# Two transformer layers on one core: the banks of the MLP down phases are copied by ScalarE and added by GpSimd's DMAs, and a fourth pair takes seven products

## The chip, the core and the metric

The kernel runs on one core of a Trainium2 chip. TensorE (PE) multiplies, VectorE (DVE) and ScalarE (ACT) work on vectors, GpSimd (POOL) and SyncE (SP) here mostly issue DMAs. The metric is the device time of one execution in microseconds, the median of several runs. A lower time is better.

## What is computed

Two different layers follow each other on x of 256 tokens by 2048 channels, all in float32. This case is about the MLP that ends each layer:

```python
x = x + jnp.square(jax.nn.relu(h @ w_mlp_up[l])) @ w_mlp_down[l]     # first_block, h = rms_norm(x)
...
u = rmsnorm(x, g_mlp) @ w_up                                          # hybrid_layer
return x + jnp.square(jax.nn.relu(u)) @ w_down
```

The hidden width is 8192. Ahead of the MLP stand, in the first layer, an attention, a gated recurrence and a short convolution, and in the second a state-space part and an attention with a top-k choice. The change leaves them alone.

## The kernel before

All weights come as one stream of 938 chunks of 512 KB (128 x 1024 floats). SP loads a chunk into one of four raw slots as soon as DVE is done with the chunk four before it. ACT rounds the chunk to `whi` (L614), and DVE makes the rest, `wlo` = raw - whi (L1104). PE multiplies with three matmuls for each product (high by high, high by low, low by high), which gives nearly float32 accuracy. `prep(c)` on ACT and on DVE always prepares chunk c+4, and whi of a chunk waits until PE is done with the chunk four before it (`mm_done`). Each engine runs its instructions in the order of the program.

An MLP is cut into four groups of hidden columns (`FF_GROUPS`), g = 0 to 3. In a group, 32 chunks make 16 hidden tiles (up), and 32 chunks multiply these with the down weights and add into X, the residual of 2 x 2048 columns. The down phase of a group (layer, g) in `SECOND_GROUPS`, six of the eight, has two halves, q = 0 and q = 1, of 16 chunks, that is 8 pairs of chunks. A half writes 1024 columns of X. A plain pair takes 24 matmuls of 512 columns (eight products, `chunk_tok`, L1991 to L1993). Other pairs use a scheme of Strassen's kind with seven products (`block_step`, L2011 to L2013), 21 matmuls. It needs sums of weight quarters, which DVE forms (`weight_sums`, L1121 to L1126, four operations on 512 columns), which ACT rounds (`sums_hi`, L618) and for which DVE makes `sums_lo` (L1109), ahead of PE's fifth product of the pair, the one into pG. DVE puts the sums ahead of the first wlo of the pair and sums_lo behind the second, and ACT's second whi waits for the sums. `BLOCK_ORDER` gives the order of the eight pairs in a half and `BLOCK_STEPS` says which of them take seven products: pairs 0 to 3 in the first half, at places 1, 3, 5 and 7, and pairs 0, 1 and 2 in the second half, at places 2, 4 and 5.

The seven-product pairs leave their results in four column banks (pO, pG, pS, pT, which the plain pairs write too) and four part banks (acc0, acc1, pV, pN). PE can start the seven-product pairs of the next half only when the part banks are read (`m_free`); it asks after the first product of the first such pair. In the kernel before, DVE does all of this: `corner` (L1519) and the evacuation at the end of the second half (L1531) add column banks, scaled by the token's norm, into X; `part_sums` copies a part bank to an SBUF tile in group 0 (L1459) and adds it there in later groups (L1457). The parts are combined in group 3 (`part_mix`, `part_add`).

GpSimd issues its DMAs in program order, at the start and between the stages. In the MLPs it has none.

Of the kernel before, what the change touches and what calls it, by code (L numbers as in the profile page):

```python
# [41 lines left out]
FF_GROUPS = 4  # L42
# [31 lines left out]

WARM = 5
COLS = 512
# [222 lines left out]
def program(nc, x, x_rows, stream, gates, gateb, finalb, params, consts, onehot, table, bias_scratch, out):  # L299
    with ExitStack() as ctx:  # L300
# [60 lines left out]
        wk = wk_f.rearrange("p (k t) -> p k t", t=T)  # L361
        tsm = sb("tsm", 48)[0]
        ssq = tsm[:, 0:16].rearrange("p (s h n) -> p s h n", s=2, h=2)
        ss = tsm[:, 16:20].rearrange("p (s h) -> p s h", s=2)
# [112 lines left out]
        xtok_landed = [ctx.enter_context(nc.semaphore(f"xtok_landed{n}")) for n in range(NG)]  # L477
        wg_landed = [ctx.enter_context(nc.semaphore(f"wg_landed{k}")) for k in range(2)]
        gb_landed = [ctx.enter_context(nc.semaphore(f"gb_landed{k}")) for k in range(2)]

# [9 lines left out]
        def phase(layer, g, q):  # L490

            return BLOCK_PHASES.index((layer, g, q)) if (layer, g, q) in BLOCK_PHASES else None

        def block_tile(p, m):
# [48 lines left out]
        def _(pool):  # L543
# [26 lines left out]
            for q in range(4):  # L570
                for n, g in enumerate(GATE_ORDER):
                    if q or n == 2:
                        pool.wait_ge(s.t_evac, 2 * G_Y + 12 * q + (-2, -8, 2)[n])
                    pool.dma_start(gbias[n % 2], gateb[:, D * g + COLS * q:D * g + COLS * q + COLS]).then_inc(gb_landed[n % 2], 16)

            pool.wait_ge(s.m_added, 8)
            pool.dma_start(fgB, finalb).then_inc(s.fg_landed, 16)
# [13 lines left out]
            for m in range(8):  # L591
                if m >= 4:
                    pool.wait_ge(s.ssd_exp, m - 3)
                pool.dma_start(cumb[:, m % 4, :], flat[2 * T * m:2 * T * m + 2 * T].unsqueeze(0).to_broadcast([P, 2 * T]))\
                    .then_inc(cumb_landed[m % 4], 16)


        @block.scalar
        def _(act):
# [198 lines left out]
            for n in range(NG):  # L798
                for j in range(8):
# [3 lines left out]
                    if j == 2:  # L803
                        if n:
                            norm_hi(1, n - 1, "g_mlp1")
                        else:
                            mix_hi(At(3))

            def mlp(b, a, i0, layer, stage, gain, before):
                for g in range(FF_GROUPS):  # L810
                    p = block_group(layer, g)

                    def up(m):
# [17 lines left out]
                        if part == 1:  # L831
                            act.wait_ge(s.mixed_made, N_BLOCK * p + m.base // 2 + 1)
                            A(mixed_hi[:, m.base // 2, :], mixed, ACT.Copy).then_inc(s.mixed_hi, 1)

                    def down(n, last):
# [25 lines left out]
                    for n in range(NG):  # L861
                        down(n, g == FF_GROUPS - 1)

# [225 lines left out]
        def _(dve):  # L1089
# [355 lines left out]
            def part_sums(layer, g, q, banks):  # L1445

                r = phase(layer, g, q)
                if banks[0] == 0:
                    dve.wait_ge(s.block_done, BLOCK_CHUNKS_AFTER[r])
                    if g:  # L1450
                        dve.wait_ge(s.m_free, 4 * phase(layer, g - 1, q) + 4)
                    elif layer:
                        dve.wait_ge(s.m_added, 8)
                for n in banks:
                    ps, part = (acc[0], acc[1], pV, pN)[n], parts[q][n]
                    if g:
                        TT(part, ps, part, ADD).then_inc(s.m_free, 1)  # L1457
                    else:
                        V.tensor_copy(part, ps).then_inc(s.m_free, 1)  # L1459

# [23 lines left out]
            def mlp(b, a, i0, layer, stage, gain):  # L1484
                for g in range(FF_GROUPS):
# [27 lines left out]
                    def down_pair(q):  # L1513
# [7 lines left out]
                        for t in range(16):  # L1521
                            if q and t in (1, 2):
                                part_sums(layer, g, 0, (0, 1) if t == 1 else (2, 3))
                            if q and t in (12, 13):
                                part_sums(layer, g, 1, (0, 1) if t == 12 else (2, 3))
                            if q and t >= 14:
                                n = 2 + t - 14
                                for h in range(2):
                                    xg = X[:, h, COLS * n:COLS * n + COLS]
                                    evac_tok(At(c + t), At(i + t - 14), h, tbanks(At(i + t - 14), True),  # L1530
                                             lambda ps: STT(xg, ps, rsq[:, h:h + 1], xg, MUL, ADD))  # L1531
                            if not q and t == 14:
                                dve.wait_ge(s.t_half, i + 1)
                                corner(0, 0)
                            if not q and t == 15:
# [1018 lines left out]
```

## Time and profile before

| | us |
|---|---|
| median of 3 runs | 2650.54 (2650.3 to 2650.7) |
| the profiled execution's own time | 2650.98 |
| its span in the profile | 2649.3 |
| PE busy | 2640.2 |
| DVE busy | 1986.9 |
| ACT busy | 1366.9 |
| POOL busy | 30.3 |

Busy time is the union of an engine's instructions in the trace. Matmuls are pipelined, so PE's records overlap and the distance between their starts tells its pace. An idle time in brackets names what ended it.

### The profile page before, as it was taken

Reading aid. Unit: us, or ns where it says so; the run is one execution under the profiler, and the core shown is the slowest. Engines: PE = TensorE matmul, PEld = TensorE weight load, DVE = VectorE, ACT = ScalarE, POOL = GpSimd, SP = SyncE. Lnnn points to the kernel's source line nnn. Section 1 sums busy time; section 2 is a strip of 40 time slices with the busy share of each in tenths; the row PEclk is TensorE's granted clock in tenths of the full one; section 3 lists DMA queues with packets and bytes.
Section 4 is the critical chain, followed back from the end, with each engine's and each line's share of the span. In section 5 each row is a group of like instructions: output and inputs, shape, how many; then the busy total and the mean of one; then the engine's idle time right before and its main releaser. Section 6 shows DMA issues by size and latency. Waiting matters only on the chain.

```text
span 2649.3 us, 39598 instructions
## 1 busy us (share of the span) xinstructions
PE 2640.2 (100%) x13478; PEld 2233.5 (84%) x13478; DVE 1986.9 (75%) x2876; ACT 1366.9 (52%) x1865; POOL 30.3 (1%) x64
## 2 busy tenths in 40 slices
PE   9999999999999999999999999999999999999999
PEld 7888888888888888888888888888788888888887
DVE  6687876555555778798797567878787978879886
ACT  6455555444444554555554454456555555455453
POOL 0100000000000000000000000000000000000000
PEclk9999999999999999999999999999999999999999
DMA  7655556665655566556566555545555655655565
GB/s 277 236 175 182 190 173 197 204 201 194 203 191 188 177 199 205 187 196 198 190 206 210 190 176 175 173 150 191 171 175 190 199 198 192 205 190 196 187 205 175
DMA packets 141721, 511.06 MB, mean 193 GB/s; under 512 B 16134, under 2 KB 16439, under 8 KB 141464
## 3 DMA queue, kind: packets, MB, share of 16 engines
q1 hardware_dynamic: 136312, 493.86, 55.9%
q0 software_dynamic: 3840, 12.86, 1.5%
q10 hardware_dynamic: 1440, 2.62, 0.3%
q8 instruction: 80, 1.31, 0.2%
q14 instruction: 49, 0.40, 0.1%
HBM read 505.08 MB, written 4.21 MB: 192 GB/s over the span
## 4 chain that ended last, share of the span: by engine, by line
PE 96%; DVE 2%; ACT 1%; DMA 0%; issue 0%; SPq 0%; ACTq 0%; DVEq 0%
PE acc L1955 26%; PE acc L1952 13%; PE acc L1973 5%; PE acc L1991 4%; PE acc L1993 4%; PE acc L1992 4%; PE pS L1991 3%; PE pS L1993 3%; PE pT L1993 3%; PE pT L1991 3%; PE pS L1992 3%; PE pT L1992 3%; PE acc L1970 2%; PE pO L1991 2%; PE pO L1993 2%; PE pG L1993 2%
## 5 line engine op out<-in xcount | busy, mean ns | idle before, releaser
L1104 DVE TENSOR_TENSOR wlo<-raw,whi 128x1024 fp32r<-128x1024 f32 x938 | 1143.4, 1223 | 446.4 <-ACT whi L614 440.5
L614 ACT ACTIVATE whi<-raw 128x1024 fp32r<-128x1024 f32 x938 | 990.0, 1057 | 793.7 <-PE pT L1993 243.1
L1955 PE MATMUL acc<-a_w,whi 128*128 128x512 f32 x2944 | 935.8, 397 | 0.1
L1952 PEld LDWEIGHTS acc<-a_w,wlo 128*128 128x128 f32 x2944 | 553.2, 188 | 129.4
L1952 PE MATMUL acc<-a_w,wlo 128*128 128x256 f32 x2944 | 578.6, 278 | 0.0
L1955 PEld LDWEIGHTS acc<-a_w,whi 128*128 128x128 f32 x2944 | 451.5, 189 | 2.5 <-DVE a_w L1157 0.8
L1973 PE MATMUL acc<-a_w,whi 128*128 128x512 f32 x592 | 198.4, 404 | 0.0
L825 ACT ACTIVATE t<-acc 128x256 f32<-128x256 f32 x128 | 48.9, 382 | 170.0 <-PE acc L1955 169.9
L1970 PEld LDWEIGHTS acc<-a_w,wlo 128*128 128x128 f32 x592 | 111.4, 188 | 24.5
L1970 PE MATMUL acc<-a_w,wlo 128*128 128x256 f32 x592 | 116.8, 279 | 0.0
L1500 DVE TENSOR_TENSOR t<-acc,t 128x256 f32<-128x256 f32 x128 | 54.0, 422 | 74.9 <-ACT t L825 74.8
L1991 PE MATMUL acc<-whi,a_w 128*128 128x512 f32 x256 | 99.9, 390 | 1.8 <-DVE wlo L1104 1.8
L1993 PE MATMUL acc<-whi,a_w 128*128 128x512 f32 x256 | 99.6, 389 | 0.0
L1992 PE MATMUL acc<-wlo,a_w 128*128 128x512 f32 x256 | 99.6, 389 | 0.0
L1973 PEld LDWEIGHTS acc<-a_w,whi 128*128 128x128 f32 x592 | 93.9, 189 | 2.3 <-issue 2.0
L1991 PE MATMUL pS<-whi,b_w 128*128 128x512 f32 x228 | 89.9, 394 | 0.0
L1993 PE MATMUL pS<-whi,b_w 128*128 128x512 f32 x228 | 88.8, 389 | 0.0
L1992 PE MATMUL pS<-wlo,b_w 128*128 128x512 f32 x228 | 88.8, 389 | 0.0
L1991 PE MATMUL pT<-whi,b_w 128*128 128x512 f32 x228 | 88.8, 389 | 0.0
L1993 PE MATMUL pT<-whi,b_w 128*128 128x512 f32 x228 | 88.7, 389 | 0.0
L1992 PE MATMUL pT<-wlo,b_w 128*128 128x512 f32 x228 | 88.7, 389 | 0.0
L1109 DVE TENSOR_TENSOR sums_lo<-sums,sums_hi 128x1536 fp32r<-128x1536 f32 x46 | 80.8, 1756 | 7.2 <-ACT sums_hi L618 7.1
(496 smaller groups left out, 3962.8 us busy)
## 6 DMA issues: line engine op xcount, KB each, us to landing
raw<-stream SPq DMA_DIRECT2D x938, 512.0 KB, 3.4
gbias<-gateb POOLq DMA_DIRECT2D x12, 256.0 KB, 4.1
X<-x_rows POOLq DMA_DIRECT2D x4, 512.0 KB, 6.8
bias_scratch<-brow POOLq DMA_DIRECT2D x8, 256.0 KB, 5.5
q<-bias_scratch POOLq DMA_DIRECT2D x8, 256.0 KB, 3.8
out<-X ACTq DMA_DIRECT2D x8, 256.0 KB, 5.3
xF<-x SPq DMA_DIRECT2D x6, 256.0 KB, 6.8
bias<-bias_scratch POOLq DMA_DIRECT2D x8, 128.0 KB, 4.1
```

Of the source, the lines that this page charges most:

```text
L614: A(whi[:, slot, :], raw[:, slot, :], ACT.Copy).then_inc(s.hi_done, 1)
L825: A(t1, acc[e.mod(2)][:, T:2 * T], ACT.Copy).then_inc(s.up_copied, 1)
L1104: TT(wlo[:, slot, :], raw[:, slot, :], whi[:, slot, :].bitcast(F32), SUB).then_inc(s.lo_done, 1)
L1109: TT(sums_lo[:, k % 2, :], sums, sums_hi[:, k % 2, :].bitcast(F32), SUB).then_inc(s.sums_lo, 1)
L1500: TT(t1, acc[e.mod(2)][:, 0:T], t1, ADD).then_inc(s.evacuated, 1)
L1952: low = lambda: MM(ps[:, 0:T], wl, wide[:, k0 + k, 0:T], start=False, stop=False, skip_group_check=True)
L1955: last = MM(ps, wh, wide[:, k0 + k, :], start=start and k == 0, stop=not start and k == KC - 1, skip_group_check=True)
L1970: low = lambda: MM(ps[:, 0:T], wl, a_w[:, m, 0:T], start=False, stop=False, skip_group_check=True)
L1973: last = MM(ps, wh, a_w[:, m, :], start=half == 0 and k == 0, stop=half == 1 and k == KC - 1, skip_group_check=True)
L1991: MM(ps, hi, wh, start=first and k == 0, stop=False)
L1992: MM(ps, hi, wl, start=False, stop=False)
L1993: end = MM(ps, lo, wh, start=False, stop=(last or (corner and h == 1)) and k == 1)
```

## The change

There are four edits.

1. `drain` is a new SBUF buffer of six tiles of 128 x 512. In the six groups' down phases ACT copies column banks (scaled by `rsq`) and part banks into its tiles (`drain_bank`), in group 0 the part banks straight to `parts`. GpSimd issues one DMA for each tile that adds it into X or into a part (`accum_op`). ACT waits for the add of six copies before. DVE's `corner`, `part_sums` and evacuations are left out there; they stay in layer 1's group 3. DVE waits for all adds in group 3 (`drains_landed`).
2. The second half takes a fourth seven-product step, pair 3, and its order is 4, 0, 1, 5, 2, 3, 6, 7: places 1, 2, 4 and 5 have seven products.
3. `dynamic_dma_scratch_size` is set to 4096.
4. `WARM`, the matmuls on zeros at the start, goes from 5 to 8.

```diff
-WARM = 5
+WARM = 8
...
+NDRAIN = 6
+DRAINS = 8 + 16 + 16
-BLOCK_ORDER = ((4, 0, 5, 1, 6, 2, 7, 3), (3, 4, 0, 5, 1, 2, 6, 7))
-BLOCK_STEPS = ((0, 1, 2, 3), (0, 1, 2))
+BLOCK_ORDER = ((4, 0, 5, 1, 6, 2, 7, 3), (4, 0, 1, 5, 2, 3, 6, 7))
+BLOCK_STEPS = ((0, 1, 2, 3), (0, 1, 2, 3))
...
+            def add(dst):
+                k = added[0]
+                added[0] += 1
+                pool.dma_start(dst, drain[:, k % NDRAIN, :], accum_op=ALU.add).then_inc(drain_added[k % NDRAIN], 16)
...
+            def add_parts(layer, g, q):
+                for n in range(4):
+                    pool.wait_ge(s.m_free, 4 * phase(layer, g, q) + n + 1)
+                    add(parts[q][n])
...
+            def drain_bank(ps, scale, freed):
+                k = drained[0]
+                drained[0] += 1
+                if k >= NDRAIN:
+                    act.wait_ge(drain_added[k % NDRAIN], 16 * (k // NDRAIN))
+                A(drain[:, k % NDRAIN, :], ps, ACT.Copy, scale=scale).then_inc(freed, 1)
...
+                        for t in range(16):
+                            if q and t == 0:
+                                drain_parts(layer, g, 0, (0, 1, 2, 3))
+                            if q and t in (12, 13):
+                                drain_parts(layer, g, 1, (0, 1) if t == 12 else (2, 3))
+                            if q and t >= 14:
+                                act.wait_ge(s.t_half, i + t - 13)
+                                column(t - 14, 0)
+                                act.wait_ge(s.mm_done, c + t + 1)
+                                column(t - 14, 1)
+                            if not q and t == 14:
...
+                                column(0, 0)
+                            if not q and t == 15:
+                                act.wait_ge(s.block_corner, p + 1)
+                                column(0, 1)
+                                act.wait_ge(s.t_half, i + 2)
+                                column(1, 0)
+                                column(1, 1)
+                            prep(At(c + t))
...
-                            if q and t in (1, 2):
-                                part_sums(layer, g, 0, (0, 1) if t == 1 else (2, 3))
-                            if q and t in (12, 13):
-                                part_sums(layer, g, 1, (0, 1) if t == 12 else (2, 3))
...
+                        if ends and m == 1:
+                            drains_landed(dve, layer)
+                            dve.wait_ge(s.t_evac, done)
...
-    nc = bacc.Bacc("TRN2", target_bir_lowering=False, num_devices=1)
+    nc = bacc.Bacc("TRN2", target_bir_lowering=False, num_devices=1, dynamic_dma_scratch_size=4096)
```

How the order moves on VectorE, at the passage from the first to the second half of group (0, 1). Before, from the sums_lo of the first half's last pair on:

```order
L1109 TENSOR_TENSOR sums_lo<-sums,sums_hi 128x1536
L1104 TENSOR_TENSOR wlo<-raw,whi 128x1024 x2
L1519 SCALAR_TENSOR_TENSOR X<-pO,tsm,X 128x512
L1104 TENSOR_TENSOR wlo<-raw,whi 128x1024
L1519 SCALAR_TENSOR_TENSOR X<-pG,tsm,X 128x512
L1519 SCALAR_TENSOR_TENSOR X<-pS,tsm,X 128x512
L1519 SCALAR_TENSOR_TENSOR X<-pT,tsm,X 128x512
L1104 TENSOR_TENSOR wlo<-raw,whi 128x1024
L1121 TENSOR_TENSOR sums<-raw 128x512
L1123 TENSOR_TENSOR sums<-raw,sums 128x512
L1124 TENSOR_TENSOR raw<-raw 128x512
L1126 TENSOR_TENSOR sums<-raw,sums 128x512
```

The same place on VectorE now:

```order
L1207 TENSOR_TENSOR sums_lo<-sums,sums_hi 128x1536
L1202 TENSOR_TENSOR wlo<-raw,whi 128x1024 x2
L1219 TENSOR_TENSOR sums<-raw 128x512
L1221 TENSOR_TENSOR sums<-raw,sums 128x512
L1222 TENSOR_TENSOR raw<-raw 128x512
L1224 TENSOR_TENSOR sums<-raw,sums 128x512
L1202 TENSOR_TENSOR wlo<-raw,whi 128x1024 x2
L1207 TENSOR_TENSOR sums_lo<-sums,sums_hi 128x1536
L1219 TENSOR_TENSOR sums<-raw 128x512
```

The four additions into X and one plain pair no longer stand ahead of the first sums, and the second pair's sums follow the first's at once.

ScalarE at the same passage, in the kernel after. `drain<-pO` to `drain<-pT` are the columns, `acc`, `pV` and `pN` the parts; before, only whi and sums_hi stood here:

```order
L661 ACTIVATE sums_hi<-sums 128x1536
L657 ACTIVATE whi<-raw 128x1024 x2
L860 ACTIVATE drain<-pO,tsm 128x512
L657 ACTIVATE whi<-raw 128x1024
L860 ACTIVATE drain<-pG,tsm 128x512
L860 ACTIVATE drain<-pS,tsm 128x512
L860 ACTIVATE drain<-pT,tsm 128x512
L657 ACTIVATE whi<-raw 128x1024
L661 ACTIVATE sums_hi<-sums 128x1536
L860 ACTIVATE drain<-acc 128x512 x2
L860 ACTIVATE drain<-pV 128x512
L860 ACTIVATE drain<-pN 128x512
```

Three of the column copies stand ahead of the whi whose pair's sums_hi follows, and the four part copies stand between that sums_hi and the next whi.

## Rows read from the trace of the kernel before

**Rows 1.** The page: span, and busy us with share and instructions.
```profile
span 2649.3 us, 39598 instructions
...
PE 2640.2 (100%) x13478; PEld 2233.5 (84%) x13478; DVE 1986.9 (75%) x2876; ACT 1366.9 (52%) x1865; POOL 30.3 (1%) x64
```

**Rows 2.** Timeline of PE, group (0, 0), down phase: start, duration, engine, line, operation.
```profile
969.15 0.39 PE L2011 MATMUL pO<-whi,b_w 128*128 128x512 f32 x1
...
979.35 0.39 PE L2011 MATMUL pO<-whi,b_w 128*128 128x512 f32 x1
...
1002.92 0.39 PE L2013 MATMUL pG<-sums_hi,b_w 128*128 128x512 f32 x1
...
1004.51 0.39 PE L1991 MATMUL pO<-whi,b_w 128*128 128x512 f32 x1
1004.74 0.39 PE L1992 MATMUL pO<-wlo,b_w 128*128 128x512 f32 x1
...
1009.95 0.39 PE L1991 MATMUL pO<-whi,b_w 128*128 128x512 f32 x1
...
1015.85 0.39 PE L2013 MATMUL pO<-whi,b_w 128*128 128x512 f32 x1
1016.28 0.50 PE L2011 MATMUL acc<-whi,b_w 128*128 128x512 f32 x1
```

**Rows 3.** Windows: the second half; busy by engine, PE clock, DMA share, GB/s.
```profile
1004.51:1046.34 41.83, 41.78 (x184) 34.27 (x183) 39.59 (x45) 19.71 (x18) 0.00 (x0) 1.00 0.62 204
```

**Rows 4.** Timeline of DVE in the same stretch.
```profile
1002.25 0.74 DVE L1519 SCALAR_TENSOR_TENSOR X<-pO,tsm,X 128x512 f32<-128x512 f32 x1
...
1015.54 0.68 DVE L1459 COPY part<-pN 128x512 f32<-128x512 f32 x1
1016.14 2.35 DVE L1104 TENSOR_TENSOR wlo<-raw,whi 128x1024 fp32r<-128x1024 f32 x2
1018.41 0.68 DVE L1121 TENSOR_TENSOR sums<-raw 128x512 f32<-128x512 f32 x1
...
1021.07 2.52 DVE L1104 TENSOR_TENSOR wlo<-raw,whi 128x1024 fp32r<-128x1024 f32 x2
1023.81 1.76 DVE L1109 TENSOR_TENSOR sums_lo<-sums,sums_hi 128x1536 fp32r<-128x1536 f32 x1 [0.22 <-ACT sums_hi L618]
1025.70 0.69 DVE L1121 TENSOR_TENSOR sums<-raw 128x512 f32<-128x512 f32 x1
...
1028.36 2.52 DVE L1104 TENSOR_TENSOR wlo<-raw,whi 128x1024 fp32r<-128x1024 f32 x2
...
1032.78 2.36 DVE L1104 TENSOR_TENSOR wlo<-raw,whi 128x1024 fp32r<-128x1024 f32 x2
```

**Rows 5.** Timeline of ACT: the whi whose raw tile came last.
```profile
1035.44 1.06 ACT L614 ACTIVATE whi<-raw 128x1024 fp32r<-128x1024 f32 x1 [1.29 <-DMA raw<-stream]
```

**Rows 6.** Groups of ACT by form: reads of a 512-column bank; busy us, mean ns.
```profile
L766 ACT ACTIVATE b_w<-pN 128x512 f32 x3 | 1.8, 588 | 0.0
...
L1009 ACT ACTIVATE vtk<-pO,f 128x512 f32<-128x512 f32 x1 | 0.7, 688 | 0.3 <-PE pO L1993 0.3
```

**Rows 7.** DMA issues of the page (KB, us to landing), and raw, 1000 to 1050.
```profile
gbias<-gateb POOLq DMA_DIRECT2D x12, 256.0 KB, 4.1
...
DMA to landing us min/median/max: 3.2/3.8/5.2
```

**Rows 8.** The start on PE: timeline, and the records of L2111 (duration ns).
```profile
1.49 6.27 PE L2111 MATMUL pV<-L 128*128 128x384 f32 x10 [1.49 <-POOL L L547]
9.53 0.47 PE L1991 MATMUL acc<-whi,a_w 128*128 128x512 f32 x1 [1.76 <-DVE wlo L1104]
...
L2111 PE MATMUL pV<-L x10: 487/844/1006, 1.5 to 7.3; 128*128 128x384 f32 x10
```

**Rows 9.** Timeline of POOL: its longest run of DMAs, and the one behind layer 0's MLP.
```profile
65.38 4.32 POOL L557 DMA_DIRECT2D bias_scratch<-brow  x8 [31.77 <-ACT brow L747]
...
1433.88 0.53 POOL L577 DMA_DIRECT2D xs<-finalb  x1 [725.46 <-DVE X L1482]
```

More of the change, by code:

```diff
@@ L362, in program @@
         tsm = sb("tsm", 48)[0]
+        drain = sb("drain", NDRAIN * COLS)[0].rearrange("p (k c) -> p k c", k=NDRAIN)
         ssq = tsm[:, 0:16].rearrange("p (s h n) -> p s h n", s=2, h=2)
@@ L492, in phase, with drains_landed @@
             return BLOCK_PHASES.index((layer, g, q)) if (layer, g, q) in BLOCK_PHASES else None
+        def drains_landed(eng, layer):
+            for k in range(NDRAIN):
+                eng.wait_ge(drain_added[k], 16 * len(range(k, DRAINS * (layer + 1), NDRAIN)))
         def block_tile(p, m):
@@ L574, in _, with add_columns, add_drains @@
                     pool.dma_start(gbias[n % 2], gateb[:, D * g + COLS * q:D * g + COLS * q + COLS]).then_inc(gb_landed[n % 2], 16)
+            added = [0]
+            def add(dst):
+                k = added[0]
+                added[0] += 1
+                pool.dma_start(dst, drain[:, k % NDRAIN, :], accum_op=ALU.add).then_inc(drain_added[k % NDRAIN], 16)
+            def add_columns(i, n):
+                for h in range(2):
+                    pool.wait_ge(s.t_evac, 2 * (i + n) + h + 1)
+                    add(X[:, h, COLS * n:COLS * n + COLS])
+            def add_parts(layer, g, q):
+                for n in range(4):
+                    pool.wait_ge(s.m_free, 4 * phase(layer, g, q) + n + 1)
+                    add(parts[q][n])
+            def add_drains(layer, i0):
+                for g in range(FF_GROUPS - 1):
+                    i = i0 + 4 * g
+                    add_columns(i, 0)
+                    add_columns(i, 1)
+                    if g:
+                        add_parts(layer, g, 0)
+                        add_parts(layer, g, 1)
+                    add_columns(i, 2)
+                    add_columns(i, 3)
+            add_drains(0, G_MLP1)
             pool.wait_ge(s.m_added, 8)
@@ L807, in _, with drain_parts @@
                             mix_hi(At(3))
+            drained = [0]
+            def drain_bank(ps, scale, freed):
[4 more added lines that the diff above has]
+                A(drain[:, k % NDRAIN, :], ps, ACT.Copy, scale=scale).then_inc(freed, 1)
+            def drain_parts(layer, g, q, banks):
+                act.wait_ge(s.block_done, BLOCK_CHUNKS_AFTER[phase(layer, g, q)])
+                if layer and not g:
+                    act.wait_ge(s.m_added, 8)
+                for n in banks:
+                    ps = (acc[0], acc[1], pV, pN)[n]
+                    if g:
+                        drain_bank(ps, 1.0, s.m_free)
+                    else:
+                        A(parts[q][n], ps, ACT.Copy).then_inc(s.m_free, 1)
             def mlp(b, a, i0, layer, stage, gain, before):
@@ L860, in mlp @@
                         up(At(15))
-                    for n in range(NG):
-                        down(n, g == FF_GROUPS - 1)
+                    if (layer, g) in SECOND_GROUPS:
+                        down_pair(0)
+                        down_pair(1)
+                    else:
+                        for n in range(NG):
+                            down(n, g == FF_GROUPS - 1)
             mlp(B_MLP1, A_MLP1, G_MLP1, 0, 1, "g_mlp1", G_OUT1 + NG - 1)
@@ L1449, in part_sums @@
                     dve.wait_ge(s.block_done, BLOCK_CHUNKS_AFTER[r])
[L1450 to L1453, printed above, removed]
+                    dve.wait_ge(s.m_free, 4 * r)
                 for n in banks:
                     ps, part = (acc[0], acc[1], pV, pN)[n], parts[q][n]
[L1456 to L1459, printed above, removed]
+                    TT(part, ps, part, ADD).then_inc(s.m_free, 1)
             def part_mix(layer, q, f):
@@ L1521, in down_pair @@
                         for t in range(16):
[L1522 to L1532 removed]
+                            if (layer, g) not in SECOND_GROUPS and t == 14:
                                 dve.wait_ge(s.t_half, i + 1)
                                 corner(0, 0)
[L1535 removed]
+                            if (layer, g) not in SECOND_GROUPS and t == 15:
                                 dve.wait_ge(s.block_corner, p + 1)
```

9 lines of the change are left out of this document (added).

## The prediction

> **What bounds the kernel now.** I read the busy line of the page first. TensorE is busy for 2640.2 of 2649.3 us [rows 1], so only what TensorE executes or waits for counts. Busy time overstates its work, though: a 512-column matmul shows 0.39 us, but the next one starts 0.227 us later [rows 2]. So I used starts, not durations. Two starts of seven-product steps in the first half are 10.20 us apart (969.15 to 979.35, one plain pair and one seven-product pair), and a plain pair takes 5.44 us (1004.51 to 1009.95) [rows 2]. A seven-product pair thus takes 4.76 us.
>
> From here T is 1004.51, the end of the first half of the down phase of group (0, 0), and times are relative to T. The other five second halves look the same in the timeline to about 0.2 us. This one lasts 41.83 us [rows 3], up to 1046.34. Five plain and three seven-product pairs make 41.48, and the remaining 0.35 us is a wait: the first step writes pO and then starts acc 0.43 us after the matmul before, when VectorE's last bank copy (pN, 1015.54) has finished [rows 2, 4]. There is no other gap of that size in the half. DVE is nearly as loaded as TensorE here, busy 39.59 of 41.83 us [rows 3]. It stays ahead because work can be four chunks early.
>
> **The matmuls.** Six second halves each lose three matmuls, 6 x 0.68 = 4.1 us. The 0.35 us wait can go too: 6 x 0.35 = 2.1. So at most 6.2 us can be won.
>
> **VectorE loses 8 bank operations of each half pair and gains a fourth weight sum.** What counts is the sequence. The order before was plain, plain, 7, plain, 7, 7, plain, plain; now it is plain, 7, 7, plain, 7, 7, plain, plain. I follow the twelve chunks of the first six pairs. From the rows: a seven-product pair costs DVE 7.29 us from its first sum to the next pair's first sum (1018.41 to 1025.70), with the first wlo 2.66, the second wlo's end 5.18 and the end of sums_lo 7.16 us after the first sum; before a plain pair the step is 7.08 (the wlo of 1032.78 against 1025.70), and a plain pair costs 2.27 (1016.14 to 1018.41) [rows 4]. Every pair of "7, 7" takes TensorE 9.5 us and DVE 14.6.
>
> The first sum can start when the wlo of the last plain pair is done, where the copy of pO starts now: T-2.26 [rows 4]. ACT then has four copies of column banks before the second whi, each 0.69 us (the scaled vtk copies) [rows 6], beginning when pG is finished at T-1.20 [rows 2]. Three of them end near T+0.8, so whi, sums_hi and DVE's sums_lo come about 0.1 us later than after an unhindered sum. The first sums of the second 7 are at T+5.14, the plain pair at 12.22, the first sums of the third at 14.49. That third pair also needs its second raw tile. Its load is issued when the wlo four chunks earlier ends (T+5.14+5.18 = 10.32). In the same pattern before, a wlo ended at 1030.88 and ACT got the tile of that slot at 1035.44, 4.56 us later [rows 4, 5]. So it arrives at T+14.88, and the fourth pair's sums start at 22.17. Its sums_lo ends at 29.33. TensorE wants the first wlo at T+25.16 and sums_lo at T+27.88. It has to wait about 1.5 us, in two portions, or 1.1 us if the raw tile is in time. **New wait: 6 x 1.5 = 9.0 us.** The second 7 is in time: its sums_lo ends at 12.3 and is wanted at 12.92. After the fourth, two plain pairs let DVE catch up, but lost TensorE time doesn't come back.
>
> **The banks on ACT.** Four plain copies follow sums_hi (done at T+3.1), 0.59 us each and 0.5 apart [rows 6], so m_free is complete near T+5.2. TensorE asks for it after 5.44 + 0.68 = T+6.12. If no copy waits for a buffer, the old 0.35 us wait is gone. From group 1 on the four are drains too, eight in a burst through six buffers: the seventh and eighth need the adds of the first and second landed. The second is issued near T-0.3. With landing time L the eighth copy starts at L-0.2; up to L = 5.7 TensorE feels nothing, and up to 6.4 the next whi is in time for DVE at T+7.80, and the lateness behind it stays 1.5. Beyond it each microsecond of L costs one in each of four halves. No row shows an add. Copies of the same 256 KB from GpSimd's queue take 4.1 us to land, and a raw load beside this work up to 5.2 [rows 7]; an add reads its target as well. I take 5 to 6, just short of the limit.
>
> The adds share the DMA engines. A 512 KB load takes 0.62 x 41.83 / 16 = 1.6 us of all engines [rows 3]. An add is 0.8 us if it costs as a copy, 1.6 if its second read counts. Between T-0.3 and T+14.9, 15.2 us, six loads (9.7) and seven adds (5.6 or 11.2) then just fit or overrun by 5.7 us. A part of this would delay that raw tile. Bounds 0 and 2 us for each of four halves, taken 0.4: **1.6 us**. It can't be a gain, since traffic is only added.
>
> The Trainium skill gives (DMA: Bandwidth & Descriptors, section on the anatomy of a GpSimd DMA) a fixed 2.0 us plus the bytes at 436 GB/s, so an estimate of 2.6 us for 256 KB; by that the ring of six never stops ACT and the sum would drop the 1.6. The 4.1 us of the rows for plain copies is longer already.
>
> **Warm-up.** Five matmuls of two records each take from 1.49 to 7.76; real work starts at 9.53 [rows 8]. Three more are six records. Their weight loads were 0.64 us apart, which would end them at 11.6 and delay everything by 2.1 us. But the last record lasts 0.49 us where the median is 0.84, so at its end it ran twice as fast, and six at 0.32 end near 9.6. The granted clock reads 1.00 there throughout (the 2.4 GHz level), and real matmuls start at 0.227 spacing at once, so nothing is gained. Taken: 0.1, bounds 0 and 2.1. The Trainium skill (TensorE: Matmul & The Clock Gate, on what is happening in the gate) says that an idle array starts at 1.2 GHz and rises after sustained work; the short last record agrees, and by it the late end would be the rarer case.
>
> **Without cost.** GpSimd idles for 725 us up to 1433.88, which covers layer 0's MLP, and the smaller scratch meets at most eight DMAs in a row, early, at 0.54 us each, with long idle time behind [rows 9]. The wait of DVE for all adds in group 3 comes four chunks (11 us) after the last one is issued and would show only if L passed 10. The edges at layer 1's last group are unchanged.
>
> **Sum.** -4.1 - 2.1 + 9.0 + 1.6 + 0.1 = +4.5 us. On the span of 2649.3 that is 2653.8; the median of the runs before is 2650.54, which is 0.44 below the profiled execution's own 2650.98. Forecast: **2655.0 us**, 0.17% more. A measurement of this kernel tells about 0.2% (5.3 us) from no change, so it is called "same", though barely.
>
> **Rivals.**
> A. DVE keeps up and the fourth step is simply won: 2644.3 to 2647. For it: DVE's sum of work in a second half falls. Against: the last four-step stretch is a plain adding up of durations that agree in all groups, and it would have to be 1.5 us too long.
> B. The adds are slow: L passes 6.4, ACT stands before the eighth buffer, m_free and whi come late. At L = 9 each of four halves costs 2.6 more, 10.4, and with it the sum is about +14.5: 2665. For it: an add reads two streams, in a burst, beside loads at 0.62 DMA share. Against: plain copies land in 4.1. It decides from L = 6.4.
> C. The warm-up ends at 11.6: +2.1 on the forecast, 2657.
> D. The scratch or the add queue does not do what is meant (GpSimd stalls for descriptors): like B, and counted there.
>
> **Chances.** Forecast mechanism, lateness of 1.1 to 2 us each half, 2650.9 to 2658: 0.55, of which 0.43 lie within 0.2% and 0.12 above. A: 0.12, of which 0.08 is faster by over 0.2% (under 2645.2). B: 0.28. C: 0.05. So faster 0.08, same 0.47, slower 0.45. The forecast's own range is 2651 to 2658; to hold 8 in 10 the whole range takes in most of A and of B: 2645.5 to 2668.
>
> **What would show it.** The first seven-product steps of a second half 5.44 us after T, with no gap before acc. The chain should run through VectorE's sums and sums_lo, with TensorE waiting at the product on pG from sums in the fourth step, about 1 us, six times. The adds' landing time should be 5 to 6 us. TensorE's first real matmul should start by 9.7. I am wrong if second halves last 40.8 us without a wait (A), or if ACT's drain copies from pN show idle time released by DMA (B). Without any new wait at all the whole account of VectorE falls.

## The result

The changed kernel takes 2670.98 us (median of six runs, 2669.7 to 2671.55) where the kernel before takes 2650.57 (2650.3 to 2650.77): the ratio is 1.0076, 95% interval 1.0064 to 1.0089. It is slower by 20.4 us. The forecast was 2655.0 and its range ended at 2668.

The page of the profiled execution (span 2669.9 us), busy lines, queues and DMA issues:

```profile
PE 2645.1 (99%) x13466; PEld 2233.1 (84%) x13466; DVE 1953.9 (73%) x2810; ACT 1424.1 (53%) x1967; POOL 100.1 (4%) x144
...
q1 hardware_dynamic: 136312, 493.86, 56.1%
q0 software_dynamic: 15360, 33.84, 5.9%
...
raw<-stream SPq DMA_DIRECT2D x938, 512.0 KB, 3.5
X<-drain POOLq DMA_DIRECT2D x48, 256.0 KB, 8.6
part<-drain POOLq DMA_DIRECT2D x32, 256.0 KB, 10.0
```

VectorE has lost 33 us of work against [rows 1] and ACT has gained 57. The adds land after 8.6 and 10.0 us; 5 to 6 was taken. Queue q0 carried 12.86 MB for 1.5% of the engines' time before. The 80 adds bring it to 5.9%, and 4.4% of 2669.9 us over 80 is **1.47 us of all 16 engines for one add of 256 KB**, in the added-up times of its packets.

The windows of the six second halves, in the columns of [rows 3]: start and end, length, busy time of PE, PEld, DVE, ACT and POOL, PE clock, DMA share, GB/s:

```profile
1004.67:1047.38 42.71, 41.37 (x181) 33.64 (x180) 35.18 (x34) 28.12 (x33) 4.18 (x6) 1.00 0.77 222
1177.36:1224.36 47.00, 43.57 (x181) 34.64 (x180) 35.14 (x34) 28.44 (x33) 11.14 (x14) 0.96 0.81 226
1354.34:1400.96 46.62, 41.91 (x181) 33.48 (x180) 35.16 (x34) 28.10 (x33) 11.36 (x14) 1.00 0.81 230
2097.94:2140.35 42.41, 41.38 (x181) 33.63 (x180) 35.19 (x34) 28.11 (x33) 4.32 (x6) 1.00 0.77 227
2270.33:2316.94 46.61, 43.54 (x181) 34.60 (x180) 35.18 (x34) 27.83 (x32) 11.14 (x13) 0.96 0.81 228
2446.91:2492.85 45.94, 41.91 (x181) 33.48 (x180) 35.18 (x34) 28.17 (x33) 11.37 (x14) 1.00 0.83 233
```

They sum to 271.29 us against 251.02 before (six times 41.81 to 41.86), so 20.27 of the 20.6 us by which the span grew lie here. Without any wait a half would last 4 x 5.44 + 4 x 4.76 = 40.80. The halves of group 0 lose 1.9 and 1.6 us, about as forecast. Those of groups 1 and 2 lose 5.1 to 6.2. They alone have four part adds beside the four column adds at their start.

What TensorE waits for in group (0, 0), from the view of waits (total, times, longest; its short gaps are partly left out):

```profile
PE pO L2096 <- DVE wlo L1202: 1.2, 1, 1.2
PE pG L2096 <- DVE sums_lo L1207: 0.2, 1, 0.2
```

And in group (0, 1), where T is 1177.36:

```profile
PE pO L2096 <- DVE wlo L1202: 2.6, 2, 2.0
PE acc L2096 <- ACT drain L860: 0.6, 1, 0.6
PE pG L2096 <- DVE sums_lo L1207: 0.2, 1, 0.2
```

Behind those waits stand DVE and ACT; DVE's timeline first, then ACT's:

```profile
1189.46 2.35 DVE L1202 TENSOR_TENSOR wlo<-raw,whi 128x1024 fp32r<-128x1024 f32 x2
1196.79 0.69 DVE L1219 TENSOR_TENSOR sums<-raw 128x512 f32<-128x512 f32 x1 [4.97 <-issue]
```

```profile
1182.34 0.60 ACT L860 ACTIVATE drain<-pV 128x512 f32<-128x512 f32 x1 [0.99 <-DMA X<-drain]
1183.63 0.60 ACT L860 ACTIVATE drain<-pN 128x512 f32<-128x512 f32 x1 [0.69 <-DMA X<-drain]
...
1195.45 1.06 ACT L657 ACTIVATE whi<-raw 128x1024 fp32r<-128x1024 f32 x1 [5.33 <-DMA raw<-stream]
```

VectorE stands 4.97 us before the sums of the third seven-product step ("issue": it waits for a landed tile, which has no releasing instruction in the view). ACT gets the pair's first tile at 1195.45, and by 1196.79, T+19.4, the second is there too; the forecast had it at T+14.9. The ring of six shows too: ACT waits 0.99 and 0.69 us for buffers, the second time for the add that GpSimd began to issue at 1177.19:

```profile
1177.19 2.63 POOL L591 DMA_DIRECT2D X<-drain  x3 [1.19 <-ACT drain L860]
```

The DMA view of 1177 to 1197 has the reason for the late tile. Its line in tenths is full from the fourth slice on, and a raw load takes 7.9 us to land (the shares add up the packets' own times, so together they can pass 100%):

```profile
DMA  5879999999998999999999999999999999999998
...
q0 software_dynamic: 1151, 2.10, 58.9%
q1 hardware_dynamic: 929, 3.40, 45.5%
...
raw<-stream SPq DMA_DIRECT2D x6, 512.0 KB, 7.9
part<-drain POOLq DMA_DIRECT2D x4, 256.0 KB, 11.0
X<-drain POOLq DMA_DIRECT2D x3, 256.0 KB, 8.4
```

### The profile page after: what moved, and what is told of

Read it like the earlier page. It is cut to its first block, busy times and chain, and to the rows that moved or that the text cites. A ratio compares the mean times of both kernels' runs of the same rounds, so it can differ in the third digit from the quotient of the medians.

```text
span 2669.9 us, 39770 instructions
## 1 busy us (share of the span) xinstructions
PE 2645.1 (99%) x13466; PEld 2233.1 (84%) x13466; DVE 1953.9 (73%) x2810; ACT 1424.1 (53%) x1967; POOL 100.1 (4%) x144
## 3 DMA queue, kind: packets, MB, share of 16 engines
q0 software_dynamic: 15360, 33.84, 5.9%
## 4 chain that ended last, share of the span: by engine, by line
PE 90%; DVE 4%; ACT 2%; DMA 2%; issue 1%; DVEq 0%; ACTq 0%; POOL 0%; SPq 0%; POOLq 0%
PE acc L2040 26%; PE acc L2037 13%; PE acc L2058 5%; PE acc L2076 4%; PE acc L2078 4%; PE acc L2077 4%; PE pS L2076 3%; PE pS L2077 3%; PE pS L2078 3%; PE pT L2076 3%; PE pT L2077 3%; PE pT L2078 3%; PE acc L2055 2%; DMA raw<-stream 2%; PE pO L2076 1%
## 5 line engine op out<-in xcount | busy, mean ns | idle before, releaser
L1207 DVE TENSOR_TENSOR sums_lo<-sums,sums_hi 128x1536 fp32r<-128x1536 f32 x52 | 91.4, 1757 | 10.2 <-ACT sums_hi L661 9.3
L2076 PE MATMUL pS<-whi,b_w 128*128 128x512 f32 x216 | 85.3, 395 | 0.0
L2078 PE MATMUL pS<-whi,b_w 128*128 128x512 f32 x216 | 84.2, 390 | 0.0
L2076 PE MATMUL pT<-whi,b_w 128*128 128x512 f32 x216 | 84.2, 390 | 0.0
L2078 PE MATMUL pT<-whi,b_w 128*128 128x512 f32 x216 | 84.1, 389 | 0.0
```

What stands on the lines that cost most here:

```text
L1207: TT(sums_lo[:, k % 2, :], sums, sums_hi[:, k % 2, :].bitcast(F32), SUB).then_inc(s.sums_lo, 1)
L2076: MM(ps, hi, wh, start=first and k == 0, stop=False)
L2078: end = MM(ps, lo, wh, start=False, stop=(last or (corner and h == 1)) and k == 1)
```

## The experiments

For each kernel "lost" is the sum of its six second halves in the profiled execution less 6 x 40.80 = 244.8 us (6 x 41.48 = 248.9 for three steps). For the kernel after it is 26.5. What a kernel loses outside these halves is not in the sum; it is under 1 us unless it is told.

**Is it the adds' bytes?** Two kernels; in the first only 8 of 512 columns are added, so X and the parts are incomplete, and in the second the DMA overwrites its target with the same 256 KB instead of adding.

```
-                pool.dma_start(dst, drain[:, k % NDRAIN, :], accum_op=ALU.add)
+e1              pool.dma_start(dst[:, 0:8], drain[:, k % NDRAIN, 0:8], accum_op=ALU.add)
+e2              pool.dma_start(dst, drain[:, k % NDRAIN, :])
```

> The changed kernel, with each add cut to its first 8 of 512 columns (4 KB instead of 256 KB; X and the parts miss the rest). Same number of DMAs, same waits. Theory (the adds' bytes fill the DMA engines and delay the raw tile of the third seven-product pair): all six second halves last like those of group 0 in the changed kernel, 42.4 to 42.7 us instead of 46 to 47 in groups 1 and 2, so 2670.9 - 4 x 4.1 = 2654.5, still about 4 above the kernel before, by VectorE's order. Rival 1 (issuing the DMAs, their count or their waits cost the time): stays near 2670. Rival 2 (VectorE's order has no cost of its own): 2645.

> The changed kernel, with plain copies of the same 256 KB in place of the adds (X and the parts get only the last drain). Theory (each add takes 1.47 us of all engines because its target is read as well; a copy should take 0.8): the overload of the window shrinks from about 6 to about 1 us, groups 1 and 2 last 43 to 44 us, in all 2656 to 2659. Rival (a DMA from GpSimd within the burst costs the loads as much whatever it does): 2667 to 2671.

Measured: 2654.94 us (ratio 1.0017, 1.0007 to 1.0026), lost 12.3; and 2656.2 (1.0019, 1.0009 to 1.0028), lost 11.1. Both times are as expected. The copies' row of q0 has the same 33.84 MB:

```profile
q0 software_dynamic: 10240, 33.84, 3.5%
```

A copy thus costs 2.0% of 2653.7 over 80, or 0.66 us of all engines, less than half an add. So 14 to 15 of the 26.5 us lost come from what an adding DMA costs above a short add or a plain copy. Some 11 to 12 us remain without it.

**Is it the fourth step?** The kernel after with the old order and three steps, and the kernel before with the new order and four.

```
+e3 (in after)   BLOCK_ORDER = (..., (3, 4, 0, 5, 1, 2, 6, 7)); BLOCK_STEPS = (..., (0, 1, 2))
+e4 (in before)  BLOCK_ORDER = (..., (4, 0, 1, 5, 2, 3, 6, 7)); BLOCK_STEPS = (..., (0, 1, 2, 3))
```

> The changed kernel, with the old order and three seven-product pairs in the second half; copies on ScalarE and adds stay. The last three matmul triples come back (+4.1), VectorE has one sum fewer. Theory: there is one more plain pair ahead of the sums, so the late raw tile costs at most 1 us a half; 2649 to 2654. Rival (the adds cost TensorE time wherever they stand): 2665 to 2672.

> The kernel before, with the new order and the fourth step only; all bank operations stay on VectorE. Theory: VectorE has 2.9 us of column additions and 2.6 us of part sums ahead of or between the first two sums; the part copies stand behind the second wlo, so TensorE waits at its first seven-product pair for m_free by about 5 us, and each half is 4 to 7 us longer than the ideal 40.8: 2668 to 2690. Rival (VectorE's order is not a bound): 2645 to 2650.

Measured: 2671.34 (1.0075, 1.0058 to 1.0092) and 2720.27 (1.026, 1.0243 to 1.0277). The first is a miss: without the fourth step the kernel is as slow. Its group (0, 0) half is free of waits (41.48), and the next one loses 5.9 us at other steps, the second and third, since these now have the late tile:

```profile
1004.73:1046.21 41.48, 41.48 (x185) 34.35 (x183) 31.82 (x31) 26.98 (x32) 4.17 (x6) 1.00 0.78 231
1176.18:1223.56 47.38, 42.88 (x184) 33.88 (x183) 31.73 (x31) 26.96 (x32) 11.17 (x13) 1.00 0.80 225
```

The second is a miss to the other side, far slower than thought: its halves last 52.5 to 54.0 us. TensorE waits in each for bank sums on VectorE (its view of waits), 58.3 us in all; most of the rest is a lower clock behind these waits, told at the end:

```profile
PE acc L2011 <- DVE part L1457: 33.0, 4, 8.3
PE acc L2011 <- DVE part L1459: 16.5, 2, 8.3
PE pG L1991 <- DVE X L1519: 8.8, 6, 1.5
```

So the first step at the second place needs the banks off VectorE, and there the change does what it should: the same wait for acc is gone in the halves of group 0 and is 0.6 us, on ScalarE's copy, in group (0, 1).

**Which adds?** The kernel after with only the part adds cut to 8 columns (parts incomplete), and the kernel after with all adds whole but those of the first half's parts issued later, one every two chunks.

```
+f1  if q == 0:
+f1      pool.wait_ge(s.mm_done, (B_MLP2 if layer else B_MLP1) + 64 * g + 48 + 6 + 2 * n)
     add(parts[q][n])
```

> The kernel after, with the adds of the four part banks (16 a group from group 1 on are then 8 full ones and 8 of 8 columns) cut to 8 columns; the adds of the column banks stay whole. Its parts are therefore incomplete. Theory (the bytes of the adds crowd the raw tile that the third seven-product step needs): with the burst at the start of a second half reduced from eight whole adds to four in groups 1 and 2, these four halves fall from 46 to 47 us to about 43.5 to 44.5, near the 42.7 and 42.4 of the group 0 halves, which have only the column adds: 2660 to 2663 us. Rival (it is the number of adds in GpSimd's queue, or their latency, not their bytes): halves of groups 1 and 2 stay above 46 us and the time above 2668.

> The kernel after; in groups 1 and 2 the four adds of the first half's part banks are no longer issued as a burst at the start of the second half but one every two chunks, from the sixth chunk on (about 15, 20, 25 and 30 us into the half). Same adds, same bytes. Theory (the burst of four column and four part adds holds up one raw tile; bytes elsewhere are free): the halves of groups 1 and 2 fall from 46 to 47 us to 42.5 to 43.5, the time to 2654 to 2657 us, as with the short part adds. Rival (the adds cost by their total, wherever they run, since the engines are near full): halves stay above 45 us, 2664 us or more.

Measured: 2655.19 (1.0015, 1.0006 to 1.0025), lost 10.7; and 2655.26 (1.0015, 1.0005 to 1.0024), lost 11.0. The first came out lower than expected: four column adds in the burst delay next to nothing in this order. The second is the decisive run. Every byte is still added, the DMA share of the half is even higher, and what groups 1 and 2 lost beyond group 0 is gone (all six halves last 42.3 to 42.9 us):

```profile
1177.02:1219.83 42.81, 41.38 (x181) 33.63 (x180) 35.10 (x34) 28.22 (x33) 11.11 (x13) 1.00 0.92 249
```

```profile
1192.25 0.69 DVE L1221 TENSOR_TENSOR sums<-raw 128x512 f32<-128x512 f32 x1 [0.78 <-issue]
```

VectorE waits 0.78 us for that tile instead of 4.97, and a share of 0.92 harms nothing where 0.81 did. ACT still waits 0.69 us for the buffer of its eighth copy, and TensorE loses nothing by it. The two windows of 1177 to 1197, after and f1, show where the difference lies, 1.05 against 0.91:

```profile
1177.00:1197.00 20.00, 19.36 (x86) 15.71 (x85) 14.20 (x15) 12.01 (x14) 6.09 (x7) 1.00 1.05 276
```

```profile
1177.00:1197.00 20.00, 20.00 (x90) 16.53 (x89) 18.29 (x19) 13.43 (x16) 3.35 (x4) 1.00 0.91 243
```

**What is the rest, 11 us?** VectorE's order, by the forecast. Order plain, 7, plain, 7, plain, 7, 7, plain; the last banks are drained two chunks later. First with the short adds (incomplete as in e1), then with the burst, then with the spaced adds.

```
+BLOCK_ORDER = ((4, 0, 5, 1, 6, 2, 7, 3), (4, 0, 5, 1, 6, 2, 3, 7))
-                            if q and t in (12, 13):
-                                drain_parts(layer, g, 1, (0, 1) if t == 12 else (2, 3))
+                            if q and t == 14:
+                                drain_parts(layer, g, 1, (0, 1, 2, 3))
```

> The same order with all adds cut to 8 columns (column banks and parts are therefore incomplete): what the order is worth when the adds move no bytes to speak of. Theory: halves of 40.8 to 41.0 us, 2643.8 to 2645.5 us; the distance to the spaced full adds is what their bytes still cost. Rival: a wait stays in each half (42 us or more, above 2650 us).

> The same order with the full adds as in the kernel after, in a burst. Theory: the order puts a plain pair before the second and third seven-product steps, which gives a late raw tile some 5 us more, so the burst costs 0 to 2 us in each of four halves: 2645 to 2655 us. Rival (the burst delays the load of any seven-product step that follows it): as in the kernel after less the 1.5 us a half, 2660 to 2663 us.

> The spaced adds, and the second half ordered plain, 7, plain, 7, plain, 7, 7, plain with its last four banks drained two chunks later. Theory (the rest of the cost, 1.5 us a half, is the pair of consecutive seven-product steps met before VectorE has a lead): halves of 40.8 to 41.5 us, 2644 to 2648 us, under the kernel before. Rival (four steps in a half are too much for VectorE or for the loads in any order): 42 us or more a half, 2652 us or more.

Measured: 2644.74 (0.9977, 0.9967 to 0.9986), lost 0.4; 2668.09 (1.0067, 1.005 to 1.0084), lost 17.7; 2669.97 (1.0065, 1.0048 to 1.0082), lost 21.1. The first is the mechanism confirmed: five of six halves last exactly 40.80 us.

```profile
1004.41:1045.21 40.80, 40.80 (x181) 33.78 (x180) 34.91 (x34) 28.00 (x33) 4.20 (x6) 1.00 0.66 206
1175.19:1215.99 40.80, 40.80 (x182) 33.78 (x181) 34.78 (x34) 27.39 (x32) 9.72 (x13) 1.00 0.69 209
```

The other two are misses. Now even group 0, with four column adds, loses 2.8 and 3.7 us with the burst. Both kernels also lose outside the halves: their spans less the six halves are 5.5 us (burst) and 9.3 us (spaced) longer than in the kernel before, in the up phases behind groups 1 and 2. There the ring of six shows: the last banks are now drained together, ScalarE's copies of pS and pT wait for the adds of parts, and the next whi, and so VectorE and TensorE, wait behind them. ACT's row in the kernel with the burst, behind layer 0's group 2:

```profile
1401.02 0.69 ACT L860 ACTIVATE drain<-pS,tsm 128x512 f32<-128x512 f32 x1 [4.97 <-DMA part<-drain]
```

Inside the halves it is a late tile again. VectorE starts the sums of the second step 8.2 us into the half in f3, with the tile in time, and 12.1 in f4, where the tile is late; f3's row stands first, f4's second:

```profile
1012.64 0.68 DVE L1219 TENSOR_TENSOR sums<-raw 128x512 f32<-128x512 f32 x1
```

```profile
1016.37 0.69 DVE L1219 TENSOR_TENSOR sums<-raw 128x512 f32<-128x512 f32 x1 [3.80 <-issue]
```

A sum that starts at 8.2 us has its sums_lo at 15.4, 3.0 us before TensorE wants it (18.4). The delay of 3.9 us passes that by 0.9, and TensorE waits 0.9 us at this step and 1.5 at the fourth. And the spacing of f1 puts adds at 15 to 30 us, where VectorE now makes the sums of the third and fourth steps (18 and 25 us): in group (0, 1) of the spaced kernel it waits 2.5 us for the tile of the second step and 2.4 for that of the third.

**Can GpSimd add by itself?** Its tensor add in place of the DMA, in the order of the change and in the new order.

```
+                nc.gpsimd.tensor_tensor(dst, dst, drain[:, k % NDRAIN, :], ALU.add)
```

> The kernel after, with each adding DMA replaced by a tensor add on GpSimd itself (same buffers, same order, same places). Theory (the adds' traffic on the DMA engines is what costs in groups 1 and 2, VectorE's order the rest): DMA share of a second half back near 0.62 to 0.65, landing of raw tiles back to 3 to 5 us, all six halves at 42.4 to 43.4 us as with the short adds, 2653 to 2657 us. Rival (GpSimd and VectorE hinder one another in SBUF, or a GpSimd add takes over 2 us so that the ring of six runs full): VectorE's 512-column operations grow beside the adds, or ACT waits for buffers, and the time is 2660 us or more.

> As the kernel with adds on GpSimd itself, and the second half's pairs ordered plain, 7, plain, 7, plain, 7, 7, plain (4, 0, 5, 1, 6, 2, 3, 7), its last four banks drained two chunks later. Theory (what is left of the cost of the fourth step is the pair of consecutive seven-product steps that comes before VectorE has any lead): only one such pair is left, behind three plain ones, so a second half takes 40.8 to 41.3 us without a wait of TensorE, and the time is 2644 to 2648 us, under the kernel before. Rival (a fourth step overloads VectorE in any order, or draining the banks later holds up the next group): halves at 42 us or more, 2652 us or more.

Measured: 2694.04 (1.0161, 1.0144 to 1.0178), lost 49.8 by the same sum, and 2676.76 (1.0098, 1.0081 to 1.0115), lost 31.8. The rival holds. GpSimd and VectorE hinder one another (timelines of e6, VectorE and GpSimd):

```profile
1178.60 1.78 DVE L1219 TENSOR_TENSOR sums<-raw 128x512 f32<-128x512 f32 x1
1180.41 0.69 DVE L1221 TENSOR_TENSOR sums<-raw,sums 128x512 f32<-128x512 f32 x1
1181.02 1.78 DVE L1222 TENSOR_TENSOR raw<-raw 128x512 f32<-128x512 f32 x1
```

```profile
1178.14 1.69 POOL L591 TENSOR_TENSOR X<-X,drain 128x512 f32<-128x512 f32 x1 [124.15 <-ACT drain L860]
1180.53 5.14 POOL L591 TENSOR_TENSOR X<-X,drain 128x512 f32<-128x512 f32 x3 [0.71 <-ACT drain L860]
```

An operation of 0.69 us takes 1.78 when it starts while GpSimd adds, and 0.69 when it starts between two of its adds.

**Warm-up and scratch alone**, in the kernel before (WARM = 8, dynamic_dma_scratch_size=4096):

> The kernel before with eight warm-up matmuls and the smaller DMA scratch alone. Theory: neither costs, first real matmul at 9.4 to 9.6 us, 2650.3 to 2651.0 us. Rival: the warm-up's end moves to 11.6 us, or GpSimd stalls for descriptors: 2652.5 us or more.

Measured: 2650.55 against 2650.64 (0.9998, 0.9989 to 1.0008). No cost shows.

**Adds behind the last tile that matters.** Eight buffers (two in tiles idle during the MLP), and no add before the second raw tile of the last seven-product step has landed. With three steps in the old order (chunk 11), and with four in the new (chunk 13):

```
+c = (B_MLP2 if layer else B_MLP1) + 64 * g + 48 + 13
+pool.wait_ge(landed[c % NSLOT], 16 * (c // NSLOT + 1))
 add_columns(i, 0)
```

> As the late adds with eight buffers, but with the order and the three seven-product steps of the kernel before: the banks' drains by ACT and DMA alone. Theory: what made the three-step kernel with drains 20 us slow (2671) is the same delayed raw tile, so with the adds behind the last one it falls to 2648 to 2650.5 us, the kernel before less its 0.35 us wait in each half. Rival (drains by ACT and DMA cost in themselves): 2655 us or more.

> Eight drain buffers instead of six (two lie in tiles that the MLP does not use), the order plain, 7, plain, 7, plain, 7, 7, plain, and no add of a half pair issued before the second raw tile of the second half's last seven-product step has landed. All adds whole. Theory (an add costs only where it delays a raw tile that VectorE's sums wait for; behind the last such tile it is free): halves of 40.8 to 41.5 us, 2644.5 to 2648 us, under the kernel before and close to the 2644.7 of the same order with short adds. Rival (the adds, now all in the last quarter of the half and in the next group's up phase, hold up ACT for buffers or the plain loads there): ACT waits for adds in front of the last four banks, TensorE waits at the start of the next group, 2652 us or more.

Measured: 2653.8 (1.001, 1.0 to 1.002), lost 0.3; one of its ten executions took 10,266 us, which I can't explain, and the median leaves it aside. And 2665.08 (1.0054, 1.0037 to 1.0071), lost 13.5. The first is above its 2648 to 2650.5, the second far above its 2644.5 to 2648. With three steps the profiled halves are free (its span is 2649.7, its median 3 us above that of before), against 2671 with the burst. Outside the halves the two lose 2.2 and 4.8 us more, which is not in the sums. With four the group 0 halves are free (40.80), and groups 1 and 2 lose 2.9 to 3.8 at their very end, where eight adds and the plain loads overrun. ACT waits for a raw tile and the bank drains stand behind it (ACT's timeline, then TensorE's wait at the next group's first matmul):

```profile
1214.02 1.06 ACT L662 ACTIVATE whi<-raw 128x1024 fp32r<-128x1024 f32 x1 [5.92 <-DMA raw<-stream]
1216.62 1.06 ACT L662 ACTIVATE whi<-raw 128x1024 fp32r<-128x1024 f32 x1 [1.54 <-DMA raw<-stream]
1217.58 1.07 ACT L865 ACTIVATE drain<-acc 128x512 f32<-128x512 f32 x2
```

```profile
PE acc L2045 <- ACT drain L865: 3.2, 1, 3.2
```

**Spreading by deadline.** With the eight buffers and the order of f3, each add is gated on a chunk's raw tile: in groups 1 and 2 two adds at chunk 7, one at 11, three at 13, one at 14, one at 15 (g3), or two at 11, three at 13, two at 14, one at 15 (g4).

```
+due[:] = [c + k for k in ((7, 7, 11, 13, 13, 13, 14, 15) if g else (13, 13, 13, 13))]
```

> As the late adds with eight buffers and the order plain, 7, plain, 7, plain, 7, 7, plain; in groups 1 and 2 the eight adds of the first half pair are no longer all issued behind the last raw tile, but two when the raw tile of chunk 7 of the second half has landed, one at chunk 11, three at 13, one at 14 and one at 15 (group 0: its four at 13, as before). Theory (an add costs when the loads and adds between two deadlines take more than the time between them; the late burst of eight overran by 3.3 us in front of the next group): the wait of 3.3 us at the start of the next group goes, halves of 40.8 to 41.8 us, 2645 to 2650 us. Rival (no place is free in groups 1 and 2: the two early adds delay the third seven-product step, or the rest still the next group): 2653 us or more.

> The same with none of the eight adds before chunk 11 has landed: two there, three at 13, two at 14, one at 15. Theory: 2 to 3 us a group are left of the 3.3 us wait at the start of the next one in groups 1 and 2 (one half of the burst is spread), 2648 to 2655 us, between the late burst and the earlier spread. Rival: as the late burst, 2660 us or more.

Measured: 2654.61 (1.0015, 1.0006 to 1.0025), lost 2.0, and 2657.65 (1.0024, 1.0013 to 1.0035), lost 8.5 in its profiled execution. Both times are above what was expected (2645 to 2650 and 2648 to 2655). The halves of g3 are nearly clean, but the loss had moved (6.5 us lie outside them): TensorE stood 1.8 and 3.3 us in the up phase of each layer's last group, behind a VectorE that waited for the last column add (waits of g3, 1390 to 1416, where TensorE's is the 1.8):

```profile
DVE part L1569 <- DMA X<-drain: 2.3, 1, 2.3
```

That is the wait which the forecast entered at no cost. In g4's profiled execution the same wait held VectorE for 6.4 us and TensorE for 5.6 in layer 0's last group, and 12.2 us of its loss lie outside the halves, which leaves part of it unexplained. The last kernel moves it and the part mixes three up tiles later:

```
-                        if ends and m == 1:
+                        if ends and m == 4:
                             drains_landed(dve, layer)
```

> As the first spread of the adds (two at chunk 7, one at 11, three at 13, one at 14, one at 15), with VectorE's wait for all adds of a layer and the part mixes behind it moved three up tiles later in the last group. In the profile of the kernel before this edit the six second halves were free of waits but for 1.2 us in all, and TensorE stood 1.8 and 3.3 us some 20 us into the last groups, behind a VectorE that had waited for the last column add. Theory (that wait is the rest of the loss): both stalls go, 2646 to 2650 us, at or under the kernel before. Rival (the last burst of eight delays the raw tiles of the next group as well, or the run-to-run spread of 6 us comes from the DMA engines elsewhere): 2652 us or more.

Measured: **2648.47 us** (2646.1 to 2652.52, 11 runs; 0.9992, 0.9983 to 1.0001), as expected; lost 2.6 in the profiled execution. It computes all and is 22 us faster than the changed kernel, but it can't be told from the kernel before.

## Why the prediction was wrong

**Matmuls (-4.1): right.** Four steps cost what the starts said, 40.80 us a half, shown exactly by f3. **The old wait (-2.1)**: gone in group 0 and in f3, replaced by 0.8 and 0.35 us of waiting for drained banks in (0, 1) and (1, 1).

**VectorE's lateness (+9.0): right in place and mechanism, a little small.** In group (0, 0) TensorE waits at the fourth seven-product pair, at pO and at pG, in two portions; the larger one is the first (1.2), where the forecast looked for about 1 us at pG. With the adds spaced (f1) it is 11.0 us in six halves, 1.8 each instead of 1.5. f3 against e1, both with short adds, shows the cause: an order with one pair of consecutive steps, late in the half, loses 0.4 us instead of 12.3.

**Warm-up (+0.1) and scratch (0): right**, by e8. The first real matmul starts at 9.43 us, 0.1 earlier than before [rows 8].

**The landing time L (5 to 6): wrong in the median, nearly right where it counted.** The median was 8.6 for the columns and 10.0 for the parts. But the ring hangs on the burst's second add, issued from 1177.19 on and landed when ACT's pN copy starts at 1183.63: 6.4 us. The forecast's own limit of 5.7 then gives TensorE a wait of 0.7, and it felt 0.8 in (0, 1), at most 0.4 in the other three halves, not 2.6 a half. ACT's wait at pN, the sign named for rival B, is there. B's direction and nearly its size came true, but most of it by another path: B put the cost into the ring.

**The contention (taken 1.6, bounds 0 and 2 us for each of four halves): this is the step that failed.** The four halves of groups 1 and 2 lost 23.0 us. Less 1.8 each for the order, 15.6 are left, 3.9 each (1.2 of the 15.6 us are waits for the ring). The working had the number in hand: six loads and seven adds in 15.2 us, over by 5.7 if the second read counts. With the measured 1.47 us an add, seven are 10.3, and 9.7 + 10.3 is 4.8 over. The tile was there at T+19.4 instead of T+14.9, 4.5 us late, and VectorE began the third step's sums with it. In group (0, 2) TensorE then stands 2.7 and 0.3 us in the third step and 1.9 and 0.4 in the fourth, 5.3 where f1 has 1.7. The view of waits has most of it:

```profile
PE pO L2096 <- DVE wlo L1202: 4.3, 2, 2.5
PE pG L2096 <- DVE sums_lo L1207: 0.4, 2, 0.2
```

But the bound was then set at 2, and 0.4 taken, and the prediction gives no reason for either. An overrun that stands in front of a tile on the critical path has to be passed on whole, less the slack of that tile, and the bound had to be 5.7 less that slack. With 3.9 in the place of 0.4, the sum would have been 4.5 - 1.6 + 15.6 = +18.5, or 2669.0, against 2671.0.

**The wait for all adds in the last group (no cost)**: right for this kernel, whose six halves hold all but 0.3 us of the loss. In g3, where the adds came later, it decided 5 us.

What stays open: g2, g3 and g5 vary from run to run by 4 to 6 us and g4 by 13, the kernel before beside them by 0.3 to 2.7. In the profiled execution of g4, its slowest (2665.4), TensorE waits 1.6 to 3.1 us for drained banks in front of each group that follows group 1 or 2, 8.5 us in all, beside the waits in the last groups. Why one execution has such waits and another of the same kernel fewer was not settled; loads that land unevenly near full engines would fit.

## What to carry to other kernels

Price an extra transfer not by its bytes over the whole phase but by the sum of transfers between its start and the next tile that a late engine needs. In the order of the change a DMA share of 0.92 was free and one of 0.81 cost 4 us a half, depending only on which 15 us held the burst. When an engine is given new work next to its own waits, look at the order before the total: VectorE had 33 us less to do and became later, because two expensive steps stood where it had no lead. And once a stall is removed, look for explicit waits for the same transfers further on; here the last 5 to 6 us lay there.

## What the hardware showed that was not expected

**An adding DMA costs 2.2 copies.** 256 KB from SBUF added into SBUF took 1.47 us of all 16 engines (1.49 in f1, where the adds are spread), a plain copy of the same tiles 0.66. GpSimd needs 0.86 us to issue one against 0.54 for the copies of before [rows 9] and those of e2.

**GpSimd's tensor add more than doubles VectorE's time.** 0.69 us became 1.78, and GpSimd's own add of 128x512 took 1.8 us in mean. The Trainium skill (SBUF — State Buffer, section on who interferes with whom) has the rule: an operation of VectorE with two SBUF inputs contends with one of GpSimd that reads SBUF. The rows of e6 agree, every stretched operation being of that form.

**TensorE's clock fell after a wait of two microseconds.** In the kernel after, group (0, 1), TensorE started nothing from 1198.5 to 1200.8. A little later its matmuls start 0.43 us apart instead of 0.227, until 1205.7; the windows show the granted clock, 0.57 being near the lower level of 1.2 GHz:

```profile
1199.00:1201.00 2.00, 0.19 (x1) 0.22 (x2) 1.93 (x3) 1.35 (x2) 0.00 (x0) 1.00 0.00 0
1201.00:1203.00 2.00, 2.00 (x8) 1.58 (x8) 1.78 (x2) 2.00 (x2) 0.00 (x0) 0.80 0.59 172
1203.00:1206.00 3.00, 3.00 (x9) 2.37 (x9) 2.83 (x4) 0.03 (x1) 0.00 (x0) 0.57 0.74 235
```

It stretched the step by 1.6 us. Little of this was lost in the end, since TensorE would have waited for VectorE anyway: its next wait is 0.8 us here and 1.9 in group (0, 2), where the clock stays at 1.00 after a wait of 2.7 us. Group (1, 1) shows the same fall after a wait of 2.2 us. So the wait before the fall doesn't decide alone, and these runs don't tell what does. After the six waits of 8.3 us in e4 the matmuls start 0.43 us apart at once, every time, for 3 to 6 us, and the granted clock reads 0.50, the lower level, from 1204 to 1209.
